# A two-layer decoder trunk on one core: the S5 read-out takes four channel tiles at a time in four column groups

## What is computed

```python
# s5_mixer: 32 channel groups of 16 channels, 64 complex states each, 256 steps
bu_r = jnp.einsum('bsgc,gpc->bsgp', ug, bbar_r)          # the drive
bu_i = jnp.einsum('bsgc,gpc->bsgp', ug, bbar_i)
_, _, xr, xi = lax.associative_scan(combine, (abar_r, abar_i, bu_r, bu_i), axis=1)
y = (jnp.einsum('bsgp,gcp->bsgc', xr, c_re)              # the read-out
     - jnp.einsum('bsgp,gcp->bsgc', xi, c_im)
     + d_skip * ug)
y = jax.nn.gelu(y.reshape(bn, s, B_WIDTH))
return y * jax.nn.sigmoid(y @ w_glu + b_glu)             # the GLU
```

## Time and profile before

| | us |
|---|---|
| median of 3 runs | 1524.16 (1523.92 to 1524.64) |
| the profiled execution, its own time | 1524.0 |
| the span within it | 1522.1 |
| TensorE busy | 1479.5 |
| VectorE busy | 1281.1 |
| ScalarE busy | 1024.4 |
| GpSimd busy | 108.4 |
| the S5 stage, from the first turn (56.09) to the end of the last scan (126.71) | 70.6 |
| start of the GLU products on TensorE | 132.66 |

### The profile page before, as it was taken

The page is one execution under the profiler, slowest core; times in us unless marked ns, Lnnn a source line. Parts: engine busy times, 40 slices in busy tenths (PEclk is TensorE's granted clock), DMA queues, the critical chain, the costliest instruction groups (busy, mean ns, idle before and its releaser), DMA issues.

```text
span 1522.1 us, 21479 instructions
## 1 busy us (share of the span) xinstructions
PE 1479.5 (97%) x7203; PEld 1153.5 (76%) x7204; DVE 1281.1 (84%) x1769; ACT 1024.4 (67%) x1314; POOL 108.4 (7%) x107
## 2 busy tenths in 40 slices
PE   4999999999999999999999999999999999999997
PEld 2645468888895588888888888888888888888886
DVE  6995458786586469999999989989989989989997
ACT  3104544443556568888888788888788888888785
POOL 5351000000000000001001001001001001001000
PEclk9999999999999999999999999999999999999999
DMA  9734968874665389999999999999999999999980
GB/s 307 292 111 144 386 248 323 305 279 140 221 210 177 112 324 393 397 367 386 391 359 384 396 353 380 396 367 371 393 370 369 393 372 366 396 374 363 396 335 30
DMA packets 209808, 482.36 MB, mean 317 GB/s; under 512 B 8084, under 2 KB 14534, under 8 KB 209622
## 3 DMA queue, kind: packets, MB, share of 16 engines
q1 hardware_dynamic: 205888, 468.91, 83.5%
q0 software_dynamic: 3216, 11.57, 2.0%
q10 hardware_dynamic: 646, 1.16, 0.3%
HBM read 473.74 MB, written 7.86 MB: 316 GB/s over the span
## 4 chain that ended last, share of the span: by engine, by line
PE 90%; DVE 2%; ACT 1%; issue 0%; DVEq 0%; ACTq 0%
PE ps L866 25%; PE ps L868 25%; PE ps L867 25%; PE ps L872 3%; PE ps L1403 2%; PE ps L1166 2%; PE ps L891 1%; PE ps L1046 1%; PE ps L1077 1%; PE ps L964 1%; PE ps L993 1%; PE ps L1137 0%; PE ps L1363 0%; DVE w_lo L2105 0%; PE ps L1354 0%
## 5 line engine op out<-in xcount | busy, mean ns | idle before, releaser
L2105 DVE TENSOR_TENSOR w_lo<-ring,w_hi 128x1024 fp32r<-128x1024 f32 (+2 forms) x572 | 670.0, 1202 | 88.2 <-ACT w_hi L1733 73.7
L1733 ACT ACTIVATE w_hi<-ring 128x1024 fp32r<-128x1024 f32 (+2 forms) x572 | 595.7, 1049 | 209.3 <-PE ps L868 204.8
L866 PE MATMUL ps<-w_hi,e_hi 128*128 128x512 f32 x896 | 355.4, 397 | 0.4 <-DVE w_lo L2105 0.3
L868 PE MATMUL ps<-w_hi,e_lo 128*128 128x512 f32 x896 | 349.6, 390 | 0.0
L867 PE MATMUL ps<-w_lo,e_hi 128*128 128x512 f32 x896 | 348.7, 389 | 0.0
L2105 DVE TENSOR_TENSOR w_lo<-ring_more,w_hi 128x1024 fp32r<-128x1024 f32 x192 | 231.7, 1223 | 15.3 <-ACT w_hi L1733 6.3
L1733 ACT ACTIVATE w_hi<-ring_more 128x1024 fp32r<-128x1024 f32 x192 | 202.7, 1060 | 47.1 <-PE ps L868 47.1
L868 PEld LDWEIGHTS ps<-w_hi,e_lo 128*128 128x128 f32 x896 | 168.2, 188 | 36.1
L866 PEld LDWEIGHTS ps<-w_hi,e_hi 128*128 128x128 f32 x896 | 168.3, 188 | 35.0 <-DVE w_lo L2105 1.6
L867 PEld LDWEIGHTS ps<-w_lo,e_hi 128*128 128x128 f32 x896 | 168.5, 188 | 32.9
L866 PE MATMUL ps<-w_hi,eT_hi 128*128 128x512 f32 x448 | 176.1, 393 | 0.0
(11 more groups left out here) (308 smaller groups left out, 1550.0 us busy)
## 6 DMA issues: line engine op xcount, KB each, us to landing
ring<-in_moe_w_gate SPq DMA_DIRECT2D x96, 1024.0 KB, 7.4
ring<-in_moe_w_up SPq DMA_DIRECT2D x80, 1024.0 KB, 7.8
ring<-in_moe_w_down SPq DMA_DIRECT2D x64, 1024.0 KB, 7.7
ring<-in_w_ada SPq DMA_DIRECT2D x24, 2048.0 KB, 12.4
ring_more<-in_moe_w_down SPq DMA_DIRECT2D x48, 1024.0 KB, 7.4
ring_more<-in_moe_w_up SPq DMA_DIRECT2D x32, 1024.0 KB, 8.0
ring_more<-in_moe_w_gate SPq DMA_DIRECT2D x16, 1024.0 KB, 7.7
ring<-in_ff_w_gate SPq DMA_DIRECT2D x5, 2048.0 KB, 8.0
```

The lines of the kernel that those rows point to most:

```text
L866: mm(o, xh, wh, start=start, stop=False)
L868: return mm(o, xl, wh, start=False, stop=stop)
L1733: fn(w, src, ACT.Copy).then_inc(hi_ready, 1)
L2105: V.tensor_tensor(w_lo[0:n, c, 0:f], src, w_hi[0:n, c, 0:f].bitcast(F32), ALU.subtract).then_inc(lo_ready, 1)
```

## The change

`read_out` takes four tiles instead of two and therefore waits for two more `post_ready`. Its loop over the four accumulating products goes over all four column groups before the next product. It is called at the end of iterations 2, 4 and 6 for tiles 0 to 3, 4 to 7 and 8 to 11, and once behind the loop for 12 to 15. The wait for `y_pre` stands in every call but the first. Nothing else is altered, and the rows on VectorE, GpSimd and ScalarE stay in their order.

```diff
--- before.py
+++ after.py
@@ -1067,12 +1067,12 @@
 
             def read_out(j0):
 
-                pe.wait_ge(post_ready, j0 + 2)
+                pe.wait_ge(post_ready, j0 + 4)
                 t = j0 // 4
-                if j0 % 4 == 0 and t >= 1:
+                if t >= 1:
                     pe.wait_ge(y_pre, t)
                 for i, (c, a, b) in enumerate(((0, 0, 0), (1, 1, 1), (2, 1, 0), (2, 0, 1))):
-                    for j in (j0, j0 + 1):
+                    for j in range(j0, j0 + 4):
                         r = slice(32 * (j % 4), 32 * (j % 4) + 32)
                         w = mm(ps[7][r, (t % 2) * S:(t % 2 + 1) * S], s5_cT[:, c, t, r], post[j % 4][:, a, b, :],
                                start=i == 0, stop=i == 3, tile_position=(0, 32 * (j % 4)))
@@ -1106,14 +1106,14 @@
                 for j in (2 * jp + 3, 2 * jp + 4):
                     if j < NCH:
                         drive(j)
-                if jp:
-                    read_out(2 * jp - 2)
+                if jp and jp % 2 == 0:
+                    read_out(2 * jp - 4)
             qk_transposes(0)
             qk_transposes(1)
             pe.wait_ge(vs_ready, 4)
             pe.wait_ge(qkT_ready, 4)
             scores_pair(0, qT, kT, 0, True)
-            read_out(NCH - 2)
+            read_out(NCH - 4)
 
             def ada_step(i):
```

## The result

The changed kernel takes 1534.13 us in the median of four runs (1533.15 to 1536.38) against 1524.04 for the kernel before in the same comparison: **slower, ratio 1.0071 with a 95% interval of 1.0058 to 1.0083**, 8.8 to 12.7 us. That is clear of the spread, though under 1%.

A forecast was written before the change was run, and what follows sets the result against it. VectorE's sixteen turns were taken to set the stage's length, with TensorE close behind. GLU delay 3.8 plus clock costs 1.2 and 1.4 gave 6.4 us, so 1530.4 profiled, 1530.6 median; range 1527.2 to 1534.0, meant to hold 8 in 10.

The forecast's parts named there:

- the third wait: VectorE's scan of tile 14: no stall; third call around 116.5 to 118.3, tile 12 ready at 120.9, place wanted about 125.
- the second wait: VectorE's scan of tile 10 waits for GpSimd's tile 8: begins 104.8 instead of 102.8, a 2.0 us stall, plus 1.2 clock.
- the end: Last scan to GLU: TensorE's 0.4 us lateness falls away, worth 0.1 to 0.3 (0.2 taken); half clock adds 1.4.
- the first wait: VectorE's scan of tile 6 waits for tile 4's place: begins at 82.6 instead of 80.62, a 2.0 us stall.
- the half clock: TensorE at 1.2 GHz behind gaps ahead of drive 12 and last read-out: 1.2 and 1.4 us; rival without cost 0.14.
- TensorE's work: Part one: a four-tile read-out in four column groups takes 1.85 us; rival, groups not side by side, 2.3 to 3.7, 0.10.
- the 2.3 worked out: Four-tile read-out by the skill page's packing speedup, an estimate: result some 1.5 us later; low end of the 0.10 groups rival.
- The relief of 7.4 us: TensorE spared four read-outs of 1.85 us; gain put at nothing since VectorE sets the stage; rival 'faster', 1516.8, 0.03.
- a gain: Rival, stalls taken up: a dozen scans each 0.1 us shorter as GpSimd idles more, 3.8 becomes 2.6, 1526.8; chance 0.08.
- the circle: Turn 9's sum (99.15), drive 12 (1.05), read-out (1.85), GpSimd's tile 8 (2.50), then VectorE's scan of tile 10 at 104.8.
- The slack of 4 us: Third call: GpSimd has tile 12 ready at 120.9, VectorE wants its place for tile 14 only at about 125.
- Handed on in full: Behind the GLU nothing takes the delay back; GLU start at 136.5 to 140 instead of 132.66, later distances as before.

The follow-up runs named there:

- the kernel with both: Against the kernel before: four-tile read-outs behind the fourth projection step, and rotary embeddings of turns 7, 8, 12 and 13 ahead of the scans; no filling products; 0.9996.
- the one with two tiles at a time: Read-outs at the change's places in the program, but each four-tile read-out cut into two of two tiles, against the kernel before; 1.0052, 1531.28 us.

## Why the prediction was wrong

The direction, the place and the kind of the loss were right; the size was not. Forecast was 6.4 us, measured 10.1 in the medians and 10.8 by the ratio, and 1534.13 lies just above the range's upper end of 1534.0. In the profiled execution, less the 0.70 by which the first turn was late, the GLU starts 11.7 us later for the 6.4, so 5.3 are missing: the third wait 1.9, the second wait with its clock 1.4, long scans less short rotary embeddings 1.4, the end 0.6, the first wait 0.3, less 0.4 in small differences. **Two steps failed: a wait was priced without the scan that follows it, and the half clock was priced only where it lay on the path itself.** Three rows of VectorE in the kernel before, on which the third of the points below rests:

```profile
86.04 0.23 DVE L2149 TENSOR_TENSOR work<-ps,cst 128x64 f32<-128x64 f32 x1
...
86.43 1.00 DVE L2151 TENSOR_TENSOR work<-work 128x64 f32<-128x64 f32 x1
...
87.85 0.80 DVE L2154 TENSOR_TENSOR work<-work 128x64 f32<-128x64 f32 x1
```

- **TensorE's work, right.** VectorE was the engine that set the stage. The read-out of four tiles takes 1.86 us at full clock (1.85 forecast), and the 2.3 worked out, as an estimate, from the Trainium skill's page "TensorE: Matmul & The Clock Gate", Part 3, is not seen here. The relief of 7.4 us came to nothing, as put.
- **The first wait, nearly right:** 2.35 for 2.0.
- **The length of the scan behind a wait, put at nothing.** The sum priced a stall as the wait alone. But the waiting scan starts when GpSimd finishes one tile, and GpSimd then starts the next at once, since its input has long been there. They run beside each other, and the scan takes 1.9 us longer, for the three scans 5.7 us in all. The trace of the kernel before held a sign of this: L2151 took 1.00 us for 64 elements a partition, with L2149 at 0.23 beside it. I read the small differences of the scans (1.27 and 1.38) as the whole of this effect and even put it down as a gain. The 1.38 of tile 6 was a small piece of it: the first of its two scans ends at 81.42, 0.55 behind a product of GpSimd that ends at 80.87. The other side of it, 4.3 us from rotary embeddings that no longer run beside GpSimd, was missing as well; in the balance the two leave 1.4 us. The long scan reaches further: with it the gap ahead of the drive of tile 10 is 2.29 us, with half clock behind it, and in the kernel that holds GpSimd back, where the scan of tile 6 takes 1.27, it is 0.31.
- **The second wait, too small.** With the clock's cost it was put at 2.0 + 1.2; it was 4.58. The drive of tile 12 took 1.75 from start to start and the read-out 3.57, both at half clock, 2.4 us more than the 2.9 in the circle. I had taken 1.2 between bounds of 0.5 and 1.95, and it was above the upper one. With the gaps filled in part, where the read-out took 2.71, the wait was 3.01; less the 0.85 that this is over 1.86, it would be some 2.2 at full clock, as an estimate, so the 2.0 were right and the price of the clock was not.
- **The third wait, put at nothing.** The reckoning let the third call come at 116.5; it came at 125.4, later by the waits before it and by an iteration at half clock. The slack of 4 us was thus used up. With the gaps filled there was no third wait. The clock was priced only where it lay on the path itself, not where it moved TensorE against the others.
- **The end, nearly right:** 1.8 us more from the last scan to the GLU, for 1.4 less 0.2. The half clock itself came as forecast, in this stage of the profiled execution with every gap of 1.4 us or more. The gaps did not: instead of 5 us ahead of the drive of tile 12 there were 2.29 ahead of tile 10's and 1.94 ahead of tile 12's, and 3.19 instead of nearly 6 ahead of the last read-out, since TensorE was itself held up by the half clock.
- **Handed on in full, right:** GLU and end moved by the same 12.4 us, though the GLU's start at 145.08 is beyond the 136.5 to 140 forecast.

By the experiments, of 10.8 us some 8 hang on the late places (1.0071 against 1.0018), and about 3.6 on the clock behind the gaps (1.0071 against 1.0047); they overlap in the part of the clock that makes the waits longer. How much each single term weighs in the median, and not in the one profiled execution, is not settled: the profiled one was 2 us slower than the median, and the runs of most kernels spread over 3 to 5 us.

## What to carry to other kernels

When a step is put off to batch it, follow the buffer that it frees, not the engine that it relieves: the relief counts only on the engine that sets the stage, and here it was another. Price a stall with what starts at its end: two engines released together by one event run beside each other, and if both work from SBUF to SBUF, one of them may pay for it. A gap on TensorE can cost twice: here the clock was at half behind four of them, and the work behind three of these came onto the path.

## What the runs showed of the hardware

- VectorE's SBUF-only operations beside a GpSimd product: two scans 3.25 us for 1.27, a 64-element operation 1.00 or 0.80 for 0.23; they end 0.55 (scan) and 0.08 us (64 elements) behind the end of a product. Operations with one operand in PSUM kept their 0.69 or 0.22 us.
- TensorE's granted clock was at 0.50 behind gaps of 1.4 to 3.2 us, with 32-row drives around some of them, and in the kernel before behind one of 0.69. The length of the gap doesn't decide alone: behind 2.58 us in the kernel with both, 0.69 ahead of a drive in the one with two tiles at a time, and 0.66 in the one with only the last call grouped, the clock stayed up. With unused products in the gaps three of the four stretches were gone.
- Four column groups with f32 operands of 128 rows run fully side by side: 32 records of 256 columns in 1.86 us, where 16 in two groups took 1.85.
